# A loop over further expert chunks: both gate-up products first, buffer waits moved behind them, one turn moved later

## The reference

```python
def hier_moe(u, p):                      # 384 tokens, 32 experts, each token goes to 2
    ...
    h = jax.nn.silu(einsum('nd,edf->nef', t, p['w_gate'])) * einsum('nd,edf->nef', t, p['w_up'])
    y = einsum('nef,efd->nd', h * comb[:, :, None], p['w_down'])
```

## Time and profile before

| | us |
|---|---|
| median of 3 runs | 1090.11 |
| lowest, highest of them | 1090.07, 1093.93 |
| the profiled execution's own time | 1091.42 |
| its span, first to last instruction | 1089.8 |

### The profile page before, as it was taken

The page is one execution under the profiler, slowest core; times in us unless marked ns, Lnnn a source line. Parts: engine busy times, 40 slices in busy tenths (PEclk is TensorE's granted clock), DMA queues, the critical chain, the costliest instruction groups (busy, mean ns, idle before and its releaser), DMA issues.

```text
span 1089.8 us, 14815 instructions
## 1 busy us (share of the span) xinstructions
PE 927.5 (85%) x5692; PEld 551.3 (51%) x5692; DVE 371.2 (34%) x915; ACT 237.4 (22%) x568; POOL 178.4 (16%) x214
## 2 busy tenths in 40 slices
PE   5999899974999876888889998998488887778886
PEld 3655465533555534454545645553355554445444
DVE  0178452255111111112527846224611111111135
ACT  2110365042111110121220026603311111012113
POOL 5000000003222222221020000000322222222200
PEclk9999999996999999999999998999699999989998
DMA  9992261295999999997995216309699999899951
GB/s 305 373 386 115 95 251 61 87 371 203 383 413 415 413 413 413 412 392 311 380 369 215 116 46 236 125 21 376 247 354 412 414 414 413 345 415 410 414 223 58
DMA packets 80900, 321.93 MB, mean 295 GB/s; under 512 B 13359, under 2 KB 25991, under 8 KB 57537
## 3 DMA queue, kind: packets, MB, share of 16 engines
q1 hardware_dynamic: 66016, 295.72, 68.7%
q0 software_dynamic: 14816, 25.29, 6.4%
HBM read 321.46 MB, written 23.59 MB: 317 GB/s over the span
## 4 chain that ended last, share of the span: by engine, by line
PE 67%; DMA 13%; DVE 7%; SPq 6%; ACT 5%; issue 2%; POOLq 0%; ACTq 0%; DVEq 0%; POOL 0%
PE ps L1169 15%; PE ps L910 11%; DMA ring<-in_w_up 8%; PE ps L1184 8%; PE ps L1122 8%; PE ps L913 4%; PE ps L885 3%; PE ps L841 2%; DMA arena<-u_rows,row_idx 2%; PE ps L1177 2%; SPq L611 2%; SPq L604 2%; DMA ring<-in_w_mod 2%; ACT arena L1435 1%; DMA y_pairs<-tail,row_idx 1%
## 5 line engine op out<-in xcount | busy, mean ns | idle before, releaser
L1169 PE MATMUL ps<-ring,tail 128*64 128x256 f32 x1760 | 205.1, 384 | 10.2 <-DMA ring<-in_w_up 8.4
L1169 PEld LDWEIGHTS ps<-ring,tail 128*64 128x64 f32 x1760 | 144.2, 139 | 83.1 <-issue 25.2
L1908 DVE TENSOR_TENSOR arena<-arena,ps 128x128 f32<-128x128 f32 x68 | 19.5, 287 | 365.3 <-ACT arena L1470 365.3
L910 PE MATMUL ps<-uT,ring 128*128 128x384 f32 x352 | 118.2, 493 | 2.0 <-ACT uT L1319 2.0
L1184 PE MATMUL ps<-ring,krow 128*64 128x512 f32 x408 | 104.8, 633 | 3.0 <-issue 2.2
L738 POOL DMA_INDIRECT y_pairs<-tail,row_idx x58 | 57.7, 994 | 289.5 <-ACT tail L1495 283.6
L910 PEld LDWEIGHTS ps<-uT,ring 128*128 128x128 f32 x352 | 67.4, 192 | 46.2 <-issue 3.4
L1495 ACT ACTIVATE tail<-ps 128x512 f32<-128x512 f32 x58 | 34.6, 597 | 190.3 <-PE ps L1184 190.3
L733 POOL DMA_INDIRECT arena<-u_rows,row_idx x66 | 68.9, 1043 | 36.3 <-issue 20.1
L1625 DVE SCALAR_TENSOR_TENSOR arena<-arena,dw 128x414 f32<-128x414 f32 x118 | 67.6, 644 | 0.0
L1470 ACT ACTIVATE arena<-ps 128x128 f32<-128x128 f32 x68 | 18.9, 278 | 214.0 <-PE ps L1169 197.2
(11 more groups left out here) (281 smaller groups left out, 1059.8 us busy)
## 6 DMA issues: line engine op xcount, KB each, us to landing
ring<-in_w_gate SPq DMA_DIRECT2D x55, 1024.0 KB, 17.9
ring<-in_w_up SPq DMA_DIRECT2D x55, 1024.0 KB, 23.8
ring<-in_w_down SPq DMA_DIRECT2D x55, 1024.0 KB, 23.5
ring<-in_w_mod SPq DMA_DIRECT2D x10, 3072.0 KB, 10.8
arena<-in_w_gate SPq DMA_DIRECT2D x13, 1024.0 KB, 16.1
arena<-in_w_up SPq DMA_DIRECT2D x13, 1024.0 KB, 19.8
arena<-in_w_down SPq DMA_DIRECT2D x13, 1024.0 KB, 19.3
ring<-in_w_in SPq DMA_DIRECT2D x8, 1536.0 KB, 17.1
```

Of the source, the lines that this page charges most:

```text
L910: last = mm(ps[:, n % 4, 0:T], slot[s][:, k, c:c + P], uT[:, k, :], start=(k == 0), stop=(k == KD - 1))
L1169: last = mm(ps[W * half:W * (half + 1), b, 0:2 * P].rearrange("p (j f) -> p j f", j=2), xc[:, b, k, :], gate_up_w[s][:, :, k, half * P:(ha ...
```

## The change

The gate-up products of p = 0 and p = 1 are issued one behind the other, and only then the hidden transposes and down products of both. ACT takes both SiLUs in the same order. The wait for the copies of main chunks moves from ahead of PE's loop to its down products; ACT's waits for stores move from ahead of its loop to its row copies; the wait for the loop's last copy moves from ahead of chunk 20's first turn to chunk 20's down product. The turn of chunk 22's rows, with DVE's copy of them, moves from the middle of chunk 20's step to its end, behind the gate-up product of chunk 21 (on DVE behind `hidden` of chunk 21). SP's and POOL's programs are not edited. No arithmetic is changed.

```diff
# tensor engine: main chunks
-                def main_chunks(first, end):
+                def main_chunks(first, end, turns=0):
...
-                        if i + 2 < end:
+                        if i + 2 < end and i != SPLIT:
                             main_x(i + 2)
+                        if i == SPLIT:
+                            pe.wait_ge(e_rows.sem, before + (turns + 2))
+                            pe.nop(nofuse=True)
...
                         if i + 1 < end:
                             main_gate_up(i + 1)
+                        if i == SPLIT:
+                            main_x(i + 2)
# tensor engine: the loop
-                wait(y_rows, l, SPLIT)
                 with pe.Fori(0, turns, 2) as r:
...
                         gate_up(p, LOOP_SLOT[p], e_gate_up)
+                    for p in range(2):
                         pe.wait_ge(e_hidden.sem, before + (r + (p + 1)))
                         tr(ps[:, 2 + 5 * p, 0:P], hrow[:, p, :], ident).then_inc(e_hturned.sem, 1)
+                        wait(y_rows, l, SPLIT - 1 + p)
...
-                pe.wait_ge(e_rows.sem, before + (turns + 2))
-                pe.nop(nofuse=True)
-                main_chunks(SPLIT, NS)
+                main_chunks(SPLIT, NS, turns)
# scalar engine: the loop
-                wait(y_stored[0], l, SPLIT // 2)
-                wait(y_stored[1], l, SPLIT // 2)
                 with act.Fori(0, turns, 2) as r:
                     for p in range(2):
                         act.wait_ge(e_gate_up.sem, before + (r + (p + 3)))
                         silu(p, e_silu)
+                    for p in range(2):
+                        wait(y_stored[p], l, SPLIT // 2)
                         act.wait_ge(e_down.sem, before + (r + (p + 3)))
# vector engine: main chunks
-                        if i + 2 < end:
+                        if i + 2 < end and i != SPLIT:
                             main_x(i + 2)
                         if i + 1 < end:
                             main_hidden(i + 1)
+                        if i == SPLIT:
+                            main_x(i + 2)
```

## The result

| | before | after |
|---|---|---|
| median of 14 runs each, us | 1091.66 | 1095.47 |
| lowest, highest | 1089.30, 1095.75 | 1092.73, 1099.97 |
| the profiled execution's own time | 1091.42 | 1092.73 |
| its span | 1089.8 | 1091.1 |

The ratio after to before is 1.0033 [1.0019, 1.0047]: slower by 3.6 us (2.1 to 5.1). The forecast was 1091.8, with a range of 1086 to 1095: right in sign, too small in size, and 0.5 us outside the range. Of the 3.7 us between the forecast and the median after, 1.55 are the median before, which came out that much higher than the one forecast from; the rest is the change.

What follows compares the result with a forecast made beforehand. The prediction took the weight loads to bound the kernel. First layer 0, second layer's first turn +1.7, second turn and behind it 0: median 1090.11 + 1.7 = 1091.8 us, range 1086 to 1095.

Steps and rivals of the forecast that it cites:

- The loads bound the kernel: Chunks of both layers: weight loads are slower than PE's 6.84 us a chunk; what counts is when the last loads land.
- First layer, sum 0: First layer's loop: 4.29 us idle becomes about 4.7 elsewhere, PE's gain goes into weight waits; sum 0, bounds gain 1.1, loss 0.5.
- The price of a chunk's loads: Chunks of both layers: 3 x 1 MB of weights at 413 GB/s take 7.6 us.
- PE's own chain: Rival, both layers' loops: PE's waits decide, so all named idle is gain, 17.6 us, giving 1072.5; chance 0.06.
- the idle DMA share: Rival, stretches of falling rate in both layers: 4.4 + 1.1 us of lost bytes come back, giving 1084.6; chance 0.09.
- Second layer, the mechanism: First turn: down of e0 waits behind e1's gate-up, so down of e2 and loads queued behind it go out 4.3 later.
- Second layer, the size: First turn: down of e2 issued at 945.5, landing at 950.5, 1.7 us later, and the loads behind it as much.
- 1.77 in all ... I take the same: Second layer, first turn: slow clock behind 3.6 us idle costs PE 1.77 us, as behind 2.81 before.
- the loads behind it ... come later by as much, since the queue is then full: Second layer: loads of e3 and chunks 20 to 30 come 1.7 us later, like down of e2, at fixed pace.
- nor is anything lost: Second layer, first turn: without the clock loss, down of e2 issued at 943.7 and 5.0 to land costs nothing.
- The price of a load on a dry queue: Second layer, down of e2: a 1 MB load on a dry queue takes 5.0 us to land.
- The rival that priced the same place higher: Second layer, first turn: both gate-ups and a down at slow clock, down of e2 6.3 late, 1096.4; chance 0.09.

Runs made afterwards that it cites:

- e8: Kernel before with up weights not loaded, gate weights standing for both (2 MB a chunk instead of 3): ratio 0.9765 to the unedited kernel before, 1068.5 us.
- e9: Changed kernel with up weights not loaded, gate weights standing for both (2 MB a chunk instead of 3): ratio 0.9685 to the unedited kernel before, 1057.2 us.
- e11: Changed kernel with SP's loop loading gate and up of both chunks before both downs, and 12 filling matmuls in PE's wait: ratio 0.9997 to the kernel before.
- e2: Changed kernel with the pair order on PE and ACT undone, moved waits and moved turn kept: ratio 0.9998 to the kernel before.
- e3: Kernel before with only the pair order in the loop on PE and ACT: ratio 1.0026.
- e1: Changed kernel with SP's loop reordered: both expert numbers read ahead, gate and up of both chunks, then both downs: ratio 1.0003 to the kernel before.
- e12: Changed kernel with 12 filling matmuls in PE's wait and down of e2 held until both downs of the turn before: ratio 1.0037 to the kernel before.
- e10: Changed kernel with SP's two reads of the expert numbers moved to the top of the loop's body: 1095.34 us, timed once.
- e5: Changed kernel with SP's load of e2's down weights waiting for both down products of the turn before: ratio 1.0039 to the kernel before.
- e7: Changed kernel, unedited, profiled and timed a second time: ratio 1.0038 to the kernel before, profiled execution 1097.47 us.
- e6: Changed kernel with 12 matmuls on constants between a turn's two gate-ups, filling PE's wait for weights: ratio 1.0003 to the kernel before.
- e4: Kernel before with only the moved turn of chunk 22 and the moved wait for the loop's last copy: ratio 1.0015.

## Why the prediction was wrong in size

- *The loads bound the kernel*: shown. Less to load took 23 to 35 us off (e8, e9). PE's gain is 9 to 11 us with the lighter loads and none with the full ones (e9, e11).
- *First layer, sum 0*: right. The idle came in another place, 5.14 us for the forecast 4.7, and the gate-up near the end started 0.18 later.
- *The price of a chunk's loads*: 7.6 us leaves out the rows that POOL moves. From 800 to 900 SP's queue moved 37.32 MB and POOL's 3.61, so the weights got 373 GB/s, and 3.15 MB at that take 8.4 us. The landing pace is thus that of all bytes together, and engines that had run ahead are not needed for it; that some of the 16 had work all along is not shown. No term of the sum rests on it.
- *PE's own chain, and the idle DMA share*: both fell. The share sank from 0.86 to 0.79 in that stretch. The Trainium skill, "Perfetto Trace Analysis", section What "DMA-bound" means, says that particular engines of the 16 may be the bound; by that the idle share is no reserve, and e2, where the share is 0.95 and nothing is gained, agrees. Which engine would bind, no run here shows.
- *Second layer, the mechanism*: right, and shown from both sides. The order alone brings the cost (e3), undoing it alone takes the cost away (e2), and so does SP following it (e1); a later load adds to it (e12).
- *Second layer, the size*: this step failed, in two of its terms. The first is "1.77 in all ... I take the same" for the slow clock. It was 0 in one profile of the change and 2.47 (6.14 - 3.67) in the other, 2.43 in e10 and 1.36 in e5: 0.7 short in e7. The second is "the loads behind it ... come later by as much, since the queue is then full". The queue wasn't full: SP had still to read e3's number and pass two waits, 1.41 us, which before had passed under other loads in the queue. Down of e2 took the forecast 5.0 to land (5.1), but up of e3 came 11.7 after its issue and not the 9.9 (953.7 + 1.7 - 945.5) that the step implies: 1.8 short. In the first profile after, without that slow clock, up of e3 was 1.8 later by the landing of up of e1 and chunk 29 1.1, where the step had "nor is anything lost". Together 1.7 + 0.7 + 1.8 = 4.2 with the slow clock; e7's trace shows 4.1, the times 3.6 (2.1 to 5.1), as a mean over executions of both kinds would. That the other runs are such a mixture is argued from the profiles and e6, not shown.
- *The price of a load on a dry queue*: 5.0 was right. The Trainium skill, "DMA: Bandwidth & Descriptors", section Anatomy of one DMA, makes it 4.4 as an estimate, by a fit for the other issue path; the trace's 5.0 and 5.1 (e7, after) are above it, and the measurement decides.
- *The range*: it stood on the median of three runs, which came out 1.5 higher with 14, and its upper end priced no queue that ran dry for longer than the slow clock made it. The rival that priced the same place higher, at 6.3, asked for both gate-ups and a down at the slow clock; the measured 3.6 lies between it and the forecast, with one gate-up and the reading on SP. That the median of 1095.5 comes near that rival's 1096.4 is in part the higher base, and so luck.

Open: the 1.0015 of e4, and why e5's time doesn't exceed e7's.

## What to carry to other kernels

Where one queue issues loads in order and each waits for a product, a new order of the products needs the same order in the queue, or the first late product holds back loads that were free to go. A gain on an engine that waits for loads elsewhere is only lent; look for the next place where it waits for the same thing before counting it. When a queue is about to run dry, count everything that its engine does between two issues, since what was free under queued loads is then paid in full.

## What the hardware showed

- The slow clock behind an idle PE came in some executions and not in others at nearly the same idle: none behind 3.74 us (gate-up 3.67, granted clock 1.00 from 930 to 950), 2.4 to 2.5 us lost behind 3.99 (e10) and 4.10 (e7, granted clock 0.50 from 940 to 944). It also came behind 2.81 in the trace before (granted clock 0.50 from 940 to 942) and behind 1.99 in e1 (gate-up of e3, 5.36 us, 0.50 from 955 to 957). The length of the idle before it alone doesn't tell it. Behind 2.76 us of matmuls on other data e6's gate-up was at full clock in the second layer, 1.43 us of idle between, and slow in the first (5.25), 2.96 between.
- SP's read of a number from memory and the waits around it took 1.41 us between two issues, 0.77 with the read made earlier.
- Landings kept the pace of 8.4 us a chunk while the mean DMA share was 0.86 (before), and at 0.79 (after) chunk 29 came only 1.1 us later by the measure of e7.
